# Hybrid pooling and latent-attention trunk on eight cores: the first two heads are prepared inside the projection of block 2, the norm runs at a fixed rate, the pooling products come one group later

## Chip, cores and metric

The kernel runs on all 8 cores of one Trainium2 chip. Each core works on its own requests and nothing is exchanged between cores. The metric is the device time of one launch in microseconds (us), that of the slowest core; lower is better.

## What is computed

The reference is a trunk of two layers. Cut to what matters here, layer 0 is:

```python
h = rms_norm(x, g) * (1 + scale) + shift            # adaLN: scale, shift from silu(cond) @ ada_w + ada_b
z = h @ w_in                                        # u (512) | cq (384) | ckv (256) | krope (32)
y_pool = pool(u) @ pool_w * pool_scale              # 4 groups, centred means over windows of 2, 4, 8, 16, minus the token
q = rms_norm((rms_norm(cq) @ w_uq) per head)        # 8 heads of 64 + 32; rotary on the last 32 for latent tokens
k, v = rms_norm(ckv) @ w_ukv                        # k: 64 + the shared 32 of krope, normalised per head
y = concat(y_pool, softmax(q k') v) @ w_out         # then x += gate * y, and a SwiGLU channel mixer
```

Layer 1 has a spatial-gating MLP in place of the mixer. A core holds 1536 tokens in three blocks of 512: block 0 is two prompts of 256 (context), blocks 1 and 2 are one latent sequence of 1024. The latent queries also see 512 cached context tokens, which the code calls key block 3. The outputs are the tokens, the normalised ckv and krope of the context.

## The kernel before

There is no compiler that orders the work. `Prog` emits instructions engine by engine in the order in which the Python code calls it, each engine runs its own in that order, and `op` (L184 to L206) attaches the semaphore waits that follow from tiles written and read. `_deps` adds one for a PSUM bank that two different engines read: the second waits for the first. All tiles lie in an arena with an allocator of its own (`new`, L50, and `drop`): a tile placed over a dropped one waits for the last use of that one. `Stream` (W) brings the weights in ten slots of 512 KB. Its DMAs are issued on the GpSimd (POOL) queue, each when `W.done` frees a slot, so they stand in one queue with POOL's arithmetic.

Order of the work: the adaLN weights and the norm of block 0; `inproj(b)` for the three blocks (L827); the preparation of heads 0 and 1 with the pooling of blocks 1 and 2; the attention of four pairs of heads (L1184), during which the next pair is prepared and 40 more pieces of `ada_w` are read and multiplied; the output projection; FFN, gMLP and FFN until the end. The work is interleaved with Python generators. A generator emits some instructions and yields, with a number that stands for the TensorE time it offers (the main one) or takes (a filler).

- `Norm.gen` (L576), 21 yields: a first one with no work; 8 squares (ACT, and POOL for every third) whose sums over the channels on TensorE follow three steps later in bank 7; the last three sums; the reciprocal root (ACT, two instructions); 8 steps of `apply`, one for each 128 channels: DVE multiplies into `xtmp` (for every fourth POOL does), ACT adds the shift and writes `hy`, which the projection of that block reads.
- `inproj(b)` has ten yields: two ckv projections, three cq projections, the krope projection (`pkr`), four tiles of u with tokens on the partitions (`u_tile`), each projection 8 matmuls of 512 columns, with the squares, sums and scalings of the two inner norms. It uses PSUM banks 0 to 5. It writes `ckvn[b]`, `cqn`, `kro` and `utok`.
- `pooling` (L910): for each of 4 groups of a block, 8 to 10 narrow matmuls of `utok` with a band matrix (the sum), its scaling out of PSUM into `pbf` (`evac`) with corrections of 8 columns at sequence ends (DVE, `icnt`), a yield, one matmul with `pool_w` (the product), its scaling into `hy`, a yield.
- `qkv(p, banks)` (L1001) prepares a pair of heads. There are six q units (192 columns for each of two token tiles; a copy into `qf`; square on POOL, `reduce` on DVE), after both units of a block `rnorm` (ACT), `rotate` (one DVE multiplication and up to five on POOL) and `turn` (8 transposes into `qT`), and for the four key blocks a k unit (2 matmuls, square on ACT, two copies into `kT`), a v unit (8 matmuls, one copy into `V`) and `sums`. `later(n, fn)` delays a step by n ticks; there is one tick for each yield.

`weave_in` (L956) gives `inproj(b)` its fillers, taken in turn against the debt: for block 0 the norm of block 1, for block 1 the norm of block 2 and the pooling of block 0, for block 2 nothing. Ahead of block b stands `drain(norms[b])`, which emits all that is left of its norm. Before the attention `weave` runs `qkv(0)` on banks 0 to 5 against the pooling of blocks 1 and 2 on banks 6 and 7 (`FB`), both scalings of the pooling on ACT. During the attention, `qkv(p + 1)` takes banks 6 and 7, which it shares with the `ada_w` pieces and the transposes of the outputs (`spread`).

## Time and profile before

| | us |
|---|---|
| median of 3 runs | 1262.86 |
| lowest of them | 1261.05 |
| the profiled execution | 1259.46 |
| its span, slowest core (core 5) | 1258.4 |
| spans of the eight cores | 1248.7 to 1258.4 |
| TensorE busy on core 5, share of the span | 1137.0, 90% |
| VectorE (DVE), ScalarE (ACT), GpSimd (POOL) busy | 480.3, 429.5, 227.8 |

All rows below are of core 5. In a timeline row the first number is the start in us, the second how long the merged instructions take from the first start to the last end; the end of a matmul includes the emptying of the array, so the next may start before it. Start to start is what a matmul costs. In brackets stands the idle time before the row and what ended it. `PEclk` is the granted TensorE clock as a share of 2.4 GHz.

### The profile page before, as it was taken

To read this page: it belongs to the slowest core of one execution; us is meant where nothing else is said; L and a number is where in the kernel's file an instruction comes from. 1 tells how busy PE (TensorE), PEld (TensorE's weight loads), DVE (VectorE), ACT (ScalarE), POOL (GpSimd) and SP (SyncE) were. 2 spreads that over 40 slices of the span, in tenths; PEclk is the share of its full clock that TensorE was granted. 3 is DMA by queue.
4 is the path that set the end of the run, shared out by engine and by line. 5 is a ranking of instruction groups with operands and counts; after the bars stand their busy time and mean duration, and the time that the engine had idled before them with its cause. 6 is when DMAs were issued, how large, how long until landed. Compare 5 with 4: busy or idle time off the path is not lost.

```text
span 1258.4 us, 17871 instructions; the slowest of 8 cores (1248.7 to 1258.4 us)
## 1 busy us (share of the span) xinstructions
PE 1137.0 (90%) x6857; PEld 547.9 (44%) x6857; DVE 480.3 (38%) x814; ACT 429.5 (34%) x669; POOL 227.8 (18%) x347
## 2 busy tenths in 40 slices
PE   2477678797889899999999999998899999999998
PEld 1233455554544344444444444444344444444443
DVE  0355673634136211152252253565622225125133
ACT  2455466665745511101101156543651110110100
POOL 3311452533213200000000022224310000000000
PEclk9988997868799899999999999998999999999999
DMA  9960318778991425225224206003533321410013
GB/s 187 239 110 1 59 30 141 112 118 130 155 167 36 67 38 92 39 35 84 34 34 84 51 1 109 1 1 49 98 55 67 68 35 34 84 17 1 1 76 126
DMA packets 24977, 90.04 MB, mean 72 GB/s; under 512 B 3392, under 2 KB 3776, under 8 KB 24128
## 3 DMA queue, kind: packets, MB, share of 16 engines
q0 software_dynamic: 21312, 77.10, 36.8%
q1 hardware_dynamic: 3584, 11.80, 2.8%
q8 instruction: 58, 0.95, 0.3%
q14 instruction: 23, 0.19, 0.1%
HBM read 153.85 MB, written 6.88 MB: 128 GB/s over the span
## 4 chain that ended last, share of the span: by engine, by line
PE 76%; DVE 7%; DMA 6%; ACT 5%; POOL 3%; issue 3%; POOLq 0%; ACTq 0%; DVEq 0%
PE pb L230 74%; DMA wslot<-w_in_u 3%; DMA wslot<-ada_w 3%; ACT pt L247 2%; DVE xtmp L268 2%; PE pb L228 2%; DVE kT L274 1%; POOL qs L251 1%; DVE xb L268 1%; DVE qf L274 1%; POOL qr L251 1%; ACT hy L247 0%; ACT xsq L247 0%; POOL qt L251 0%; DVE utok L251 0%
## 5 line engine op out<-in xcount | busy, mean ns | idle before, releaser
L230 PE MATMUL pb<-hb,wslotx 128*128 128x512 bf16 x1440 | 319.9, 379 | 0.0
L247 ACT ACTIVATE sg<-pb 128x512 f32<-128x512 f32 x132 | 78.7, 596 | 472.0 <-PE pb L230 472.0
L251 DVE TENSOR_TENSOR apart<-pb,sg 128x512 bf16<-128x512 f32 x132 | 91.3, 691 | 369.0 <-PE pb L230 346.2
L230 PEld LDWEIGHTS pb<-hb,wslotx 128*128 128x128 bf16 x1440 | 140.8, 98 | 170.0 <-issue 0.3
L268 DVE SCALAR_TENSOR_TENSOR xb<-pb,mod,xb 128x512 f32<-128x512 f32 x192 | 143.6, 749 | 143.1 <-PE pb L230 143.1
L230 PE MATMUL pb<-hb,wslot 128*128 128x512 bf16 x864 | 197.6, 385 | 0.0
L230 PE MATMUL pb<-apart,wslot 128*128 128x512 bf16 x768 | 167.1, 379 | 0.0
L247 ACT ACTIVATE pt<-pb,rk 128x1024 bf16<-128x1024 f32 (+1 forms) x128 | 118.9, 953 | 58.0 <-PE pb L230 57.2
L230 PEld LDWEIGHTS pb<-hb,wslot 128*128 128x128 bf16 x864 | 85.6, 99 | 104.9 <-issue 5.7
L230 PEld LDWEIGHTS pb<-apart,wslot 128*128 128x128 bf16 x768 | 75.1, 98 | 90.2
L230 PE MATMUL pb<-hy,wslot 128*128 128x512 bf16 (+1 forms) x336 | 82.4, 397 | 4.7 <-ACT hy L247 4.5
L230 PE MATMUL pb<-qT,kT 96*128 96x512 bf16 (+1 forms) x224 | 80.5, 449 | 1.6 <-issue 1.6
L268 DVE SCALAR_TENSOR_TENSOR xtmp<-xb,AA,xrs 128x512 f32<-128x512 f32 x72 | 62.5, 906 | 9.8 <-ACT xrs L247 9.4
L228 PEld LDWEIGHTS pb<-V,pt 128*128 128x128 bf16 x768 | 39.5, 109 | 59.7 <-issue 54.5
L247 ACT ACTIVATE xsq<-xb 128x512 bf16<-128x512 f32 x72 | 41.8, 621 | 65.4 <-PE pb L230 36.3
L230 PE MATMUL pb<-apart,wslotx 128*128 128x512 bf16 x288 | 62.5, 379 | 0.0
L230 PE MATMUL pb<-xsq,ones 128*128 128x512 bf16 x96 | 30.0, 405 | 32.0 <-ACT xsq L247 24.2
L228 PE MATMUL pb<-V,pt 128*128 128x65 bf16 x768 | 47.0, 212 | 12.2 <-ACT pt L247 10.7
L251 POOL TENSOR_TENSOR xtmp<-xb,xrs 128x512 f32<-128x512 f32 x24 | 33.6, 1402 | 124.6 <-ACT hb L247 85.4
L230 PEld LDWEIGHTS pb<-hy,wslot 128*128 128x128 bf16 (+1 forms) x336 | 33.4, 101 | 49.0 <-issue 14.8
L247 ACT ACTIVATE hb<-xtmp,mod 128x512 bf16<-128x512 f32 x54 | 37.6, 720 | 33.1 <-DVE xtmp L268 33.1
L230 PE MATMUL pb<-scT,wslot 128*128 128x2 bf16 x768 | 26.9, 165 | 21.5 <-DMA wslot<-ada_w 20.0
(130 smaller groups left out, 953.8 us busy)
## 6 DMA issues: line engine op xcount, KB each, us to landing
wslot<-ada_w POOLq DMA_DIRECT2D x48, 512.0 KB, 10.1
wslot<-ffn_wd POOLq DMA_DIRECT2D x16, 512.0 KB, 9.9
wslotx<-ffn_wu POOLq DMA_DIRECT2D x14, 512.0 KB, 10.6
wslotx<-ffn_wg POOLq DMA_DIRECT2D x12, 512.0 KB, 18.9
y<-xb SPq DMA_DIRECT2D x12, 512.0 KB, 2.7
wslot<-ffn_wg POOLq DMA_DIRECT2D x10, 512.0 KB, 7.4
xb<-x_in POOLq DMA_DIRECT2D x4, 1024.0 KB, 41.7
wslot<-ffn_wu POOLq DMA_DIRECT2D x8, 512.0 KB, 7.5
```

Of the source, the lines that this page charges most:

```text
L228: return self.op("pe", lambda g: g.matmul(out, lhsT, rhs, start=start, stop=stop, skip_group_check=True), [lhsT, rhs], [out], inc=inc)
L230: return self.op("pe", lambda g: g.matmul(out, lhsT, rhs, start=start, stop=stop), [lhsT, rhs], [out], inc=inc)
L247: return self.op("act", lambda g: g.activation(out=out, in_=in_, func=func, bias=bias, scale=scale), reads, [out])
L251: return self.op(e, lambda g: g.tensor_tensor(out=out, in0=in0, in1=in1, op=op), [in0, in1], [out])
L268: return self.op(e, lambda g: g.scalar_tensor_tensor(out=out, in0=in0, scalar=sc, in1=in1, op0=op0, op1=op1), reads, [out])
L274: return self.op(e, lambda g: g.tensor_copy(out=out, in_=in_), [in_], [out])
```

## The change

- `inproj(2)` now has `qkv(0)` as its filler: 12 of its steps, which are 12 of the 14 units. The tiles for it are made before block 2, and `qkv(0)` takes banks 6 and 7 there and banks 0 to 5 afterwards (`bk0`). For p = 0 `qf` is copied by ACT, no longer by DVE.
- `weave_in` and its debt are replaced by `together(main, n, parts)`: a part with k steps gives k/n steps for each of the n yields of main. The norm of block 1 runs at 26 steps on 10 yields, the norm of block 2 at 36 on 10, the pooling of block 0 at 9 on 10. The latter two are drained after block 1.
- `pooling` emits a product one group behind its sum where it has two banks. Of blocks 1 and 2 the `pbf` scaling moves from ACT to DVE; the scaling into `hy` stays on ACT.
- `qkv` is written as a list of units. The order is new for the later pairs too: q and k or v units alternate, where six q units stood ahead of all k and v units. The two `rotate` of a block come one tick apart, where both came in one. The copies of the rotary keys into `kT` (SP's DMAs) are issued for p = 0 after block 2.
- To make room in the arena: `Norm` has two `xrs` tiles for three blocks, `ckr_f` is dropped early, `in_kv` and `in_q0` are given back in the middle of block 2, and the allocator takes the tightest gap, no longer the first, in the whole kernel.

```diff
-        addr = gaps[-1][1] - nbytes if high else gaps[0][0]
+        addr = gaps[-1][1] - nbytes if high else min(gaps, key=lambda g: (g[1] - g[0], g[0]))[0]
...
-                self.rs = [new("xrs%d" % i, [128, 512], F32) for i in range(3)]
+                self.rs = [new("xrs%d" % i, [128, 512], F32) for i in range(2)]
+                self.rs.append(self.rs[0])
...
+            if b == 2:
+                W.done("in_kv")
+                W.done("in_q0")
             pq.append(proj(5, W.get("in_q1"), 0))
...
         def pooling(blocks, banks, step, evac):
+            late = collections.deque()
+            lag = len(banks) - 1
+            def product(b, g, pbf):
+                ps2 = P.bank(banks)
+                P.mm(ps2[:], pw[:, g, :], pbf[:])
+                evac[1](hy[b][:, g, :], ps2[:], vecs[:, 128 + g:129 + g])
...
-                    evac(pbf[:], ps[:], 1.0 / w)
+                    evac[0](pbf[:], ps[:], 1.0 / w)
...
                     yield step
-                    ps2 = P.bank(banks)
-                    P.mm(ps2[:], pw[:, g, :], pbf[:])
-                    evac(hy[b][:, g, :], ps2[:], vecs[:, 128 + g:129 + g])
-                    yield step
+                    late.append((b, g, pbf))
+                    if len(late) > lag:
+                        product(*late.popleft())
+                        yield step
...
+            while late:
+                product(*late.popleft())
+                yield step
...
-        for b in range(3):
-            drain(norms[b])
-            fill = collections.deque()
-            if b < 2:
-                fill.append(norms[b + 1])
-            if b > 0:
-                fill.append(pooling([b - 1] if b == 1 else [], (6,), 1.3, lambda o, i, sc: P.ts("dve", o, i, sc, None, ALU.mult)))
-            weave_in(inproj(b), fill)
...
-                    P.cp("dve", qf[:].rearrange("p a d -> p (a d)"), ps[:, 0:384])
-                    later(3 - u + 1, functools.partial(rotate, b, u, qf, qt, sr))
+                P.cp("act" if p == 0 else "dve", qf[:].rearrange("p a d -> p (a d)"), ps[:, 0:384])
                 later(1, functools.partial(reduce, ss, u, qs))
+                if u == 1:
+                    later(2, functools.partial(rnorm, ss, sr))
+                    for v in range(2):
+                        later(3 + v, functools.partial(rotate, b, v, qts[v][0], qts[v][1], sr))
+                    later(6, functools.partial(turn, b, [x[1] for x in qts]))
...
-            for kb in (3, 0, 1, 2):
...
+            order = [("q", 0, 0), ("q", 0, 1), ("k", 3), ("v", 3), ("q", 1, 0), ("q", 1, 1), ("k", 0), ("v", 0), ("k", 1), ("v", 1),
+                     ("q", 2, 0), ("q", 2, 1), ("k", 2), ("v", 2)] if p == 0 else [("q", 0, 0), ("k", 3), ("q", 0, 1), ("v", 3), ("q", 1, 0), ("k", 0), ("q", 1, 1), ("v", 0),
+                     ("q", 2, 0), ("k", 1), ("q", 2, 1), ("v", 1), ("k", 2), ("v", 2)]
+            for kind, *arg in order:
+                {"q": q_unit, "k": k_unit, "v": v_unit}[kind](*arg)
                 yield 0.5
                 tick()
...
+        def together(main, n, parts):
+            for i, _ in enumerate(main):
+                for g, k in parts:
+                    for _ in range((i + 1) * k // n - i * k // n):
+                        next(g, None)
+        drain(norms[0])
+        together(inproj(0), 10, [(norms[1], 26)])
+        drain(norms[1])
+        pool0 = pooling([0], (6,), 1.3, (on_dve, on_dve))
+        together(inproj(1), 10, [(norms[2], 36), (pool0, 9)])
+        drain(norms[2])
+        drain(pool0)
...
+        bk0 = [FB]
+        q0 = qkv(0, bk0)
+        together(inproj(2), 10, [(q0, 12)])
+        for key in ("in_u0", "in_u1", "in_q1"):
+            W.done(key)
...
-        q0 = qkv(0, (0, 1, 2, 3, 4, 5))
-        weave(q0, collections.deque([pooling([1, 2], FB, 0.5, lambda o, i, sc: P.act(o, i, AF.Copy, scale=sc))]), flush=True)
+        bk0[0] = (0, 1, 2, 3, 4, 5)
+        together(pooling([1, 2], FB, 0.5, (on_dve, on_act)), 16, [(q0, 9)])
+        drain(q0)
```

## Rows read from the trace of the kernel before

**Rows 1.** The page, granted TensorE clock in 40 slices of 31.5 us, tenths.

```profile
PEclk9988997868799899999999999998999999999999
```

**Rows 2.** Busy time by stretch: PE, PEld, DVE, ACT, POOL, clock, DMA share, GB/s.

```profile
80.90:107.70 26.80, 23.76 (x138) 11.22 (x134) 16.67 (x39) 12.71 (x23) 1.04 (x1) 1.00 0.10 15
107.70:136.80 29.10, 24.07 (x95) 9.43 (x96) 12.71 (x19) 15.06 (x24) 3.61 (x3) 0.82 0.04 5
136.80:166.40 29.60, 17.58 (x199) 13.64 (x197) 20.22 (x45) 15.49 (x31) 16.38 (x34) 0.88 0.34 63
166.40:358.80 192.40, 158.08 (x2085) 98.72 (x2085) 81.84 (x208) 131.31 (x167) 71.36 (x140) 0.81 0.78 122
358.80:1258.40 899.60, 879.87 (x4112) 399.62 (x4112) 328.97 (x459) 224.44 (x379) 109.34 (x130) 0.99 0.29 53
```

**Rows 3.** TensorE's waits, 107.7 to 166.4 us: total, times, longest.

```profile
PE pb L230 <- DVE pbf L251: 9.2, 5, 3.1
PE pb L230 <- ACT hy L247: 4.5, 3, 3.3
```

**Rows 4.** TensorE's timeline where block 2 begins.

```profile
106.87 0.81 PE L230 MATMUL pb<-xsq,ones 128*128 128x512 bf16 x3
110.97 1.91 PE L230 MATMUL pb<-hy,wslot 128*128 128x512 bf16 x3 [3.29 <-ACT hy L247]
113.51 2.42 PE L230 MATMUL pb<-hy,wslot 128*128 128x512 bf16 x4 [0.63 <-ACT hy L247]
116.51 6.12 PE L230 MATMUL pb<-hy,wslot 128*128 128x512 bf16 x17 [0.58 <-ACT hy L247]
```

**Rows 5.** TensorE's timeline, matmuls at full clock, one after the other.

```profile
142.32 0.66 PE L230 MATMUL pb<-wslot,cqn 128*128 128x192 bf16 x6
142.81 0.66 PE L228 MATMUL pb<-band,utok 128*128 128x132 bf16 x10
143.33 0.66 PE L230 MATMUL pb<-wslot,cqn 128*128 128x192 bf16 x6
...
182.10 0.63 PE L239 MATMUL pb<-ident,qt 128*96 128x128 bf16 x8 [1.17 <-DVE kT L274]
182.57 0.61 PE L230 MATMUL pb<-wslot,ckvn 128*128 128x128 bf16 x8
183.02 0.60 PE L230 MATMUL pb<-qT,kT 96*128 96x512 bf16 x2
...
359.59 15.70 PE L230 MATMUL pb<-hy,wslot 128*128 128x512 bf16 x72
```

**Rows 6.** Groups, 60 to 170 us: line, engine, operation, count, busy us, mean ns.

```profile
L268 DVE SCALAR_TENSOR_TENSOR xtmp<-xb,AA,xrs 128x512 f32<-128x512 f32 x12 | 9.6, 839 | 0.4 <-ACT xrs L247 0.3
L274 DVE COPY qf<-pb 128x384 f32<-128x384 f32 x8 | 4.4, 547 | 1.1 <-PE pb L230 1.1
L259 DVE TENSOR_SCALAR pbf<-pb 128x512 bf16<-128x512 f32 x4 | 2.8, 692 | 2.9 <-PE pb L228 2.9
L247 ACT ACTIVATE pbf<-pb 128x512 bf16<-128x512 f32 x8 | 4.7, 588 | 1.5 <-PE pb L228 1.3
```

**Rows 7.** TensorE's waits during the attention, 166.4 to 358.8 us.

```profile
PE pb L228 <- ACT pt L247: 10.7, 28, 0.8
PE pb L239 <- DVE kT L274: 6.3, 5, 1.5
PE pb L230 <- DVE kT L274: 4.1, 5, 1.1
```

**Rows 8.** Busy time in four stretches of the attention, columns as in group 2.

```profile
193.00:206.00 13.00, 12.84 (x132) 7.08 (x129) 4.12 (x14) 8.25 (x10) 1.59 (x3) 0.50 1.04 159
244.00:269.00 25.00, 23.94 (x256) 13.23 (x255) 4.91 (x18) 17.45 (x19) 2.12 (x4) 0.50 0.94 149
306.00:332.00 26.00, 24.78 (x263) 13.87 (x264) 3.87 (x16) 18.07 (x23) 3.41 (x7) 0.50 1.00 158
333.00:358.00 25.00, 18.46 (x276) 9.62 (x272) 1.76 (x8) 22.62 (x21) 6.34 (x12) 1.00 0.98 155
```

More of the change, by code:

```diff
@@ L825, in build @@
         key_sums(3)
+        drop(ckr_f)
         def inproj(b):
@@ L1004, in qkv @@
             kT, qT, V, rk = d["kT"], d["qT"], d["V"], d["rk"]
-            for hl in range(2):
-                P.dma("sp", kT[64:96, hl, :], kro[64:96, :], "kro%d" % (p % 2))
+            if p > 0:
+                rotary_keys(p)
             lag = collections.deque()
@@ L1023, in turn @@
             def turn(b, qts):
-                ps = P.bank(banks).bitcast(BF16)
+                ps = P.bank(banks[0]).bitcast(BF16)
                 for hl in range(2):
@@ new lines, in q_unit @@
+            def q_unit(b, u):
+                if u == 0:
+                    qst[b] = (ssr.next(), ssr.next(), [])
+                ss, sr, qts = qst[b]
+                ps = P.bank(banks[0])
+                for i in range(2):
+                    t = 4 * b + 2 * u + i
+                    P.mmg(ps[:, i * 192:(i + 1) * 192], [(cqn[:, kc, t * 128:(t + 1) * 128], wuq[kc][:, p * 192:(p + 1) * 192]) for kc in range(3)])
+                qf = qfr.next()
+                qs = qsr.next()
+                qt = qtr.next()
+                qts.append((qf, qt))
+                P.cp("act" if p == 0 else "dve", qf[:].rearrange("p a d -> p (a d)"), ps[:, 0:384])
+                P.tt("pool", qs[:], qf[:], qf[:], ALU.mult)
+                later(1, functools.partial(reduce, ss, u, qs))
+                if u == 1:
[3 more added lines that the diff above has]
+                    later(6, functools.partial(turn, b, [x[1] for x in qts]))
@@ L1077, in qkv, with sums @@
             ksb = new("ksb", [128, 16, 2], F32)
-            pend = None
-            def sums():
-                kb, sq = pend
-                ps = P.bank(banks)
+            def sums(kb, sq):
+                ps = P.bank(banks[0])
                 for i in range(4):
@@ L1086, in sums, with k_unit @@
                 P.tt("dve", ksb[:, kb * 4:kb * 4 + 4, :], ps[:, 0:8].rearrange("p (a b) -> p a b", b=2), k_bc, ALU.add)
-            for kb in (3, 0, 1, 2):
-                ps = P.bank(banks)
-                lw = [wukv[:, kc, p * 256:p * 256 + 128] for kc in range(2)]
-                P.mmg(ps[:], [(lw[kc], ckvn[kb][:, kc, :]) for kc in range(2)])
+            def k_unit(kb):
+                ps = P.bank(banks[0])
+                P.mmg(ps[:], [(wukv[:, kc, p * 256:p * 256 + 128], ckvn[kb][:, kc, :]) for kc in range(2)])
                 sq = sqk.next()
@@ L1095, in qkv, with v_unit, krstd @@
                     P.cp("act" if p == 0 and hl == 1 else "dve", kT[0:64, hl, blk(kb)], ps[hl * 64:hl * 64 + 64, :])
[L1096 to L1098 removed]
+                later(2, functools.partial(sums, kb, sq))
+            def v_unit(kb):
+                ps = P.bank(banks[0])
                 for i in range(4):
[L1100 to L1101 removed]
+                    P.mmg(ps[:, i * 128:(i + 1) * 128],
+                          [(ckvn[kb][:, kc, i * 128:(i + 1) * 128], wukv[:, kc, p * 256 + 128:p * 256 + 256]) for kc in range(2)])
                 P.cp("dve", V[:, kb * 4:kb * 4 + 4, :, 0:64], ps[:].rearrange("p (t h d) -> p t h d", t=4, h=2))
+            def krstd():
+                P.act(ksb[:], ksb[:], AF.Ln, bias=epsc[:, 3:4])
+                P.act(rk[:], ksb[:], AF.Exp, scale=-0.5)
+                drop(ksb)
+            qst = {}
+            order = [("q", 0, 0), ("q", 0, 1), ("k", 3), ("v", 3), ("q", 1, 0), ("q", 1, 1), ("k", 0), ("v", 0), ("k", 1), ("v", 1),
[3 more added lines that the diff above has]
+                {"q": q_unit, "k": k_unit, "v": v_unit}[kind](*arg)
                 yield 0.5
                 tick()
[L1105 to L1112 removed]
+            later(2, krstd)
             while lag:
@@ L1115, in qkv @@
                 tick()
+        def together(main, n, parts):
[3 more added lines that the diff above has]
+                        next(g, None)
+        on_dve = lambda o, i, sc: P.ts("dve", o, i, sc, None, ALU.mult)
+        on_act = lambda o, i, sc: P.act(o, i, AF.Copy, scale=sc)
+        drain(norms[0])
[5 more added lines that the diff above has]
+        drain(pool0)
+        N.close()
+        drop(*held)
+        wukv = W.get("ukv")
+        wuq = [W.get("uq0")[:, 0, :], W.get("uq0")[:, 1, :], W.get("uq1")[:, 0, :]]
+        kvq = [new_kvq(0)]
+        qfr = Ring([new("qf%d" % i, [128, 4, 96], F32) for i in range(5)])
+        qsr = Ring([new("qs%d" % i, [128, 4, 96], F32) for i in range(2)])
+        qtr = Ring([new("qt%d" % i, [128, 4, 96], BF16) for i in range(6)])
+        qrr = Ring([new("qr%d" % i, [128, 2, 4, 32], F32) for i in range(2)])
+        sqk = Ring([new("sqk%d" % i, [128, 512], BF16) for i in range(2)])
+        ssr = Ring([new("ss%d" % i, [128, 8], F32) for i in range(4)])
+        bk0 = [FB]
[3 more added lines that the diff above has]
+            W.done(key)
+        drop(*sqb.t, *rsb.t, *t2k.t, sqkr, ropek)
+        rotary_keys(0)
+        ptr = Ring([new("pt%d" % i, [128, 1024], BF16) for i in range(3)])
+        rdr = Ring([new("rd%d" % i, [128, 4], F32) for i in range(2)])
         def ada_gen():
@@ L1218, in before @@
             drain(nxt[0])
-            nxt[0] = qkv(p + 1, FB) if p < 3 else iter(())
+            nxt[0] = qkv(p + 1, [FB]) if p < 3 else iter(())
         debt = 0.0
```

56 lines of the change are left out of this document (5 added, 51 removed).

## The prediction

> **What bounds the kernel now.** I read the clock line of the page first, then the busy time by stretch, then TensorE's waits in the stretches that the change touches, and last the timeline where they fall. The last 899.6 us, from the output projection on, have TensorE busy for 879.87 at a clock of 0.99 [rows 2], and the change leaves their order alone: they are fixed. The clock line has its low digits from the third slice to the eleventh [rows 1]. What can move is three stretches ahead of the attention and the attention itself. From 80.9 to 107.7 us runs the projection of block 1 (26.8 us, clock 1.00). From 107.7 to 136.8 runs block 2 (29.1 us, clock 0.82), from 136.8 to 166.4 the first preparation with the pooling (29.6 us, TensorE busy 17.58), and then 192.4 us of attention at a clock of 0.81 [rows 2].
>
> Two waits stand out in the 58.7 us from 107.7 on [rows 3]. TensorE waits 4.5 us for `hy`: the norm of block 2 isn't ready when block 1 is, since two fillers shared the debt, and `drain` emits what is left of it in one piece. TensorE waits 9.2 us for `pbf`: a pooling product stands directly behind its own sum, and TensorE takes its queue in order, so the q and k units behind it stand too. After the first of the two waits the matmuls of block 2 run at half clock: 17 in 6.12 us, 0.36 each [rows 4], where 72 take 15.70, 0.22 each [rows 5].
>
> **What TensorE must do.** Prices, start to start: a matmul of 512 columns 15.70/72 = 0.218; a q unit 142.81 - 142.32 = 0.49; a pooling sum 143.33 - 142.81 = 0.52; a turn 182.57 - 182.10 = 0.47; a v unit 183.02 - 182.57 = 0.45; a k unit two matmuls of 512, 0.44 [rows 5]. I put 0.12 for four sums of two columns (estimate, a quarter of the 8 narrow matmuls of a v unit). The projection of a block has 80 matmuls of 512 columns and 5 for its inner norms: 85 x 0.218 = 18.5.
> - Block 1: 18.5, with 8 norm sums 1.7 and the pooling of block 0, 4 x (0.52 + 0.22) = 3.0: 23.2.
> - Block 2, with 12 steps of `qkv(0)`: 18.5, six q units 2.9, three k and three v units 2.7, two turns 0.9, three sums 0.4: 25.4.
> - Pooling stage: 8 x 0.74 = 5.9, one k and one v unit 0.9, one turn 0.5, one sum 0.1: 7.4.
>
> Together 56.0, where 85.5 pass now. A gain of 29.5 is thus the bound from above for this part. None of the arithmetic goes away; only idle time and half clock do.
>
> **Block 1 becomes longer.** At 3.6 steps a yield the norm is through its squares in three yields and through its 8 `apply` in the fourth to sixth: up to 4 in one yield, 3 of them on DVE at 0.84 [rows 6], 2.5 us, beside the scalings of the block and of the pooling, against some 2.2 us of TensorE. So DVE falls behind by about 4 us there. The pooling of block 0 has one bank (6), its product waits for DVE's `pbf` and its next sum for DVE's `hy`: these stand behind the `apply` in DVE's queue, and all later projections stand behind them in TensorE's. I count two such waits of 1.5 to 2.2 us and two of about 0.6: 5, on top of 23.2 and of some 1.3 that stay as they are: 29.5. Bounds: 25 if DVE's other idle time takes it all up; 33 if most of the norm's rest, which now shows as 9 us of delay between 107.7 and 116.5 [rows 4], returns inside the block. Over the block DVE has 16.67 + 6 x 0.84 = 21.7 us of work in it, so it doesn't bound the whole.
>
> **Block 2 takes in the preparation.** What goes: the wait of 3.29 with its 0.63 and 0.58, and the half clock, 24 matmuls at 0.14 more than 0.22 each, 3.4 us [rows 4]. What comes: 6.9 us of units. On two banks each unit waits until the one two before it is out of PSUM; a unit lasts a yield of 2.4 us, and a k unit needs a square on ACT and two copies one after the other, about 2 us. So most waits are covered. A turn stands behind POOL's rotations, about 2.2 us each for latent tokens, and these have two ticks: I give 1 us of waiting for that, 2 for the banks. 25.4 + 3.1 = 28.5. Bounds: 26 and 32. The copies of `qf` on ACT take 6 x 0.55 from DVE. If ACT is late, TensorE's squares of `sqb` are, and they are of the next inner norm only. POOL's queue holds three weight DMAs at the end of block 2, as now; their pieces are wanted by the attention, 14 us later.
>
> **The pooling stage.** With the product one group behind, TensorE no longer waits for the `pbf` just made, but sums and products still alternate over two banks, so that every sum has the same bank as the sum before. A group costs the sum 0.52, its scaling on DVE 0.69 [rows 6], a correction and the hand-overs 0.3: 1.5; eight make 12. DVE has some 5 us of `qkv(0)` to do in between, of which 3 fit beside the sums that TensorE makes meanwhile: I take 14. Bounds: 12 and 18. `pbf` on ACT costs 0.59 [rows 6], so the move itself is a loss of 0.1 a group, made up by the saved hand-over between ACT's scaling and DVE's correction. The key copies on SP are issued at the end of block 2 and have the whole stage to land.
>
> Sum: 29.5 + 28.5 + 14 = 72.0 for 85.5, a gain of 13.5; from the bounds 25 + 26 + 12 and 33 + 32 + 18, between 22.5 and 2.5. DVE's total of 49.6 over the three stretches [rows 2] goes up by 8 x 0.69 and down by 6 x 0.55, to 51.8, still below 72.
>
> **The attention.** The diff also reorders the later pairs. Now a k unit, a v unit and a turn come close together on banks 6 and 7, and TensorE waits for the copies of `kT` for 6.3 + 4.1 = 10.4 us [rows 7]; the 6.3 are all turns, as the one of 1.17 ahead of 182.10 [rows 5]. In the new order the turns come due at ticks 8, 12 and 16, behind v units, and three of four k units are followed by a q unit. The turns' waits should go; the 4.1 stay, since an `ada_w` piece between two units takes a bank as well. In these stretches TensorE is the late one, so a wait saved there is time saved: 6. Bounds: -3 (the waits turn up behind `qf` instead, which has a DVE copy too, and prep ends later by its tail of 2 yields) and 16 (below). The weight stream is not in the way: 192 us carry 40 pieces, 4.8 us each.
>
> **Clock in the attention.** Three stretches of 13, 25 and 26 us run at half clock with TensorE busy 95% and more of the time, and in the timeline each comes soon after a pair's k units; in the last 25 us, at full clock, TensorE idles 6.5 of 25 and keeps the clock [rows 8]. At half clock a step costs about 1.6, in comparable steps at full clock 1.25 (estimate, from 13 and 7 steps that I counted in the timeline): 64 us at half clock cost 14. If what costs the clock is the waits of the k units, part of the 14 comes back. The Trainium skill (TensorE: Matmul & The Clock Gate, "A second HAM failure mode: psum-queue depth-cycling") says that a kernel that cycles through PSUM banks, with short idle times between groups of matmuls, loses and regains the clock again and again. By that rule the low stretches stay, for the short waits stay, and the attention gives 6 at most; the last stretch of rows 8 speaks against it. I leave the clock as it is in the sum and make its return a rival.
>
> **Allocator and the rest.** Tightest gap for first gap changes which freed tile a new one waits for. After the attention TensorE needs its first FFN weights about 40 us later, so a DMA that starts up to ten us later is hidden; without that cover it would show as a wait for `wslotx`. Two `xrs` for three blocks: block 2's root waits for block 0's last `apply`, a whole block earlier. Nothing for both, bounds -2 and 2.
>
> **Sum.** 1259.46 (profiled execution, span 1258.4 and 1.1 around it) - 13.5 - 6 = 1240. The median of the runs shown is 3.4 above the profiled execution, the lowest 1.6 above; I put 2 on it: **1242**.
>
> **The rivals.**
> - *The idle time only moves (19%).* DVE's backlog in block 1 and the two-bank chains keep what the waits gave up: front 5, attention 2, time 1254. For it: DVE's 20.22 of 29.6 us [rows 2] already come from such chains. Against it: each of the two waits of rows 3 has a cause that the diff removes.
> - *The attention's clock comes back (17%).* 10 of the 14 us, with 19.5: 1232; with a good front stage 1226. For it: the low stretches follow the k units. Against it: they might as well follow from the load that comes later, and the rule above.
> - *Slower (4%).* In block 1, or behind a turn in block 2, TensorE waits 3 us and more in one piece, as ahead of 110.97, and the clock falls to 1.2 GHz there and is not regained because the waits recur. Block 2 and the pooling stage with half of block 1 are 44 us of TensorE work at full clock. Doubled, less the 12 us of waits that it swallows, that costs 32 and gives 1242 + 32 = 1274. It decides from 27 us of work at half clock on, where the 19.5 are used up. For it: 3.29 us of waiting did cost the clock [rows 4]. Against it: the longest single wait I count is 2.2.
> - *It doesn't do what it says (5%).* Block 2's norm is drained late all the same, as ACT and DVE take their queues in order; then front 2 and attention 2, time 1257.
> - *As forecast (55%)*, own range 1233 to 1250.
>
> **How the numbers follow.** 1225 is the rival of the clock with a good front stage, 1256 reaches past the idle time that only moves; outside lie the slower case, half of the one that does nothing and the ends of the others. 2% is 25 us, about what a measurement of this kernel can tell from no change: the line is at 1237.6. Below it lie the rival of the clock and a quarter of the forecast: 0.30. Above 1288 lies little of the slower case, but its price is uncertain: 0.03. The rest, 0.67, is within.
>
> **What the profile after would show.** Right: no `hy` wait of over 1 us where block 2 begins, clock 1.00 through block 2; first scores of the attention near 153 us, not 166.5; block 1 longer by 2 to 3 us with waits for DVE's `pbf` and `hy`; the `pbf` wait in the pooling stage replaced by sums that wait for DVE's `pbf` of the sum before, under 1 us each; no turns that wait for `kT`. Wrong: scores later than 160; attention longer than 190; a new wait for POOL's `qt` of some us. The forecast is wrong as a whole if the part from 358.8 on changes by more than 3.

## The result, and the profile after

The changed kernel takes 1272.82 us against 1261.05 in the same comparison (medians of five runs each). In some launches the cores of one die ran longer at a lower clock; the ratios leave these launches out, the medians include them. The ratio is 1.009, 95% interval 1.0076 to 1.0103: slower by under 2%, but clearly slower. The forecast was 1242, with a range of 1225 to 1256: wrong in sign and outside the range. The slowest core's span is 1272.9 us where it was 1258.4.

The page's clock line answers to [rows 1]. The fourth digit, with block 2 in it, is 9 where it was 8. The sixth to the eleventh, most of the attention, are 7, 8, 7, 6, 9 and 5, where they were 9, 7, 8, 6, 8 and 7:

```profile
PEclk9989978769599999999999999999999999999999
```

Busy time by stretch on core 6, the slowest, columns as in [rows 2]. The cuts are the key sums of blocks 0, 1 and 2, the first score and the first transposes behind the attention. (In [rows 2] the two cuts after blocks 1 and 2 lie 0.9 and 0.6 us behind the key sums.)

```profile
81.20:112.50 31.30, 24.07 (x134) 11.11 (x136) 20.04 (x45) 19.72 (x33) 3.76 (x4) 1.00 0.08 13
112.50:139.10 26.60, 24.44 (x158) 12.84 (x160) 14.83 (x28) 14.30 (x28) 6.99 (x13) 1.00 0.00 1
139.10:163.60 24.50, 13.85 (x135) 10.34 (x136) 15.42 (x34) 8.46 (x16) 9.21 (x21) 0.82 0.47 78
163.60:372.20 208.60, 166.33 (x2074) 106.62 (x2084) 79.43 (x207) 131.00 (x165) 68.60 (x138) 0.75 0.68 113
372.20:1272.90 900.70, 875.90 (x4029) 399.81 (x4112) 330.24 (x461) 224.41 (x379) 110.25 (x132) 0.99 0.28 53
```

Three things are to be seen. Block 2 follows block 1 at full clock, with the preparation of pair 0 inside. The stage behind it still lasts 24.5 us, with TensorE busy for 13.85. And the attention, 192.4 us before at a clock of 0.81 [rows 2], is 208.6 here at 0.75. The last stretch is 900.7 for 899.6: it didn't change.

The wait where block 2 began [rows 4] is gone. This is TensorE's timeline around that place, with the first q unit of pair 0 behind the first projection:

```profile
112.43 0.24 PE L230 MATMUL pb<-ones,sqkr 128*128 128x1 bf16 x4
112.54 1.89 PE L230 MATMUL pb<-hy,wslot 128*128 128x512 bf16 x8
114.61 0.66 PE L230 MATMUL pb<-wslot,cqn 128*128 128x192 bf16 x6 [0.19 <-DVE hy L259]
```

TensorE's waits in block 1, 81.2 to 112.5 us: total, times, longest. Before, the stretch had only 1.7 for `hy` and some for the band's DMA.

```profile
PE pb L230 <- DVE pbf L251: 2.8, 3, 1.2
PE pb L228 <- DVE hy L259: 2.3, 2, 1.6
PE pb L230 <- ACT hy L247: 0.9, 1, 0.9
PE pb L230 <- ACT rsb L247: 0.6, 1, 0.6
```

The same from the key sums of block 2 to the first score, 139.1 to 163.6 us. The 9.2 us for `pbf` [rows 3] are 2.2 + 0.6 now, but a copy of `V`, a turn and `hy` have taken their place:

```profile
PE pb L230 <- DVE V L274: 3.6, 1, 3.6
PE pb L239 <- POOL qt L251: 2.5, 3, 1.8
PE pb L228 <- DVE pbf L251: 2.2, 4, 0.8
PE pb L230 <- ACT hy L247: 1.5, 2, 1.2
PE pb L230 <- DVE pbf L251: 0.6, 1, 0.6
```

The longest of them, on TensorE and on DVE. The q unit that starts at 142.99 needs the bank that the copy of `V` empties, and DVE does the rotary keys of block 2 first:

```profile
142.99 0.66 PE L230 MATMUL pb<-wslot,cqn 128*128 128x192 bf16 x6 [3.57 <-DVE V L274]
139.40 1.54 DVE L268 SCALAR_TENSOR_TENSOR t2k<-pb,vecs,ropek 32x512 f32<-32x512 f32 x2
140.97 0.68 DVE L251 TENSOR_TENSOR kro<-t2k,t2k 32x512 bf16<-32x512 f32 x1
141.69 0.42 DVE L251 TENSOR_TENSOR qt<-qf,ss 128x256 bf16<-128x256 f32 x1
142.15 0.69 DVE L274 CAST V<-pb 128x512 bf16<-128x512 f32 x1
```

And in the attention, 163.6 to 372.2 us, against [rows 7]. The turns no longer wait for `kT`, they wait for POOL:

```profile
PE pb L228 <- ACT pt L247: 9.6, 27, 0.7
PE pb L239 <- POOL qt L251: 8.9, 6, 2.6
PE pb L230 <- DVE kT L274: 6.6, 6, 1.2
PE pb L230 <- DMA wslot<-ada_w: 4.2, 5, 1.5
PE pb L239 <- DVE mod L251: 3.4, 4, 1.9
PE pb L230 <- DVE ksb L251: 2.4, 4, 0.7
```

To compare kernels I took the same cuts on all eight cores and averaged: from the key sums of block 0 to those of block 1, from there to those of block 2, from there to the first score, and the attention from its first to its last exponential. "Half clock" is twice the attention's length times (1 - its mean granted clock), the time it would be at 1.2 GHz if it is at 2.4 otherwise; "busy" and "waits" are TensorE's in the attention. The runs are described further below.

| kernel | block 1 | block 2 | stage behind | attention | half clock | busy | waits | ratio to before (95%) |
|---|---|---|---|---|---|---|---|---|
| before | 26.2 | 29.2 | 30.7 | 187.4 | 55 | 150.5 | 34.9 | |
| changed | 31.1 | 26.6 | 24.6 | 201.5 | 85 | 158.9 | 40.7 | 1.009 (1.0076, 1.0103) |
| e1 old pairs | 31.1 | 26.6 | 24.6 | 187.3 | 53 | 149.6 | 35.6 | 0.9956 (0.9940, 0.9971) |
| e2 new pairs alone | 26.3 | 29.3 | 30.5 | 200.1 | 79 | 156.6 | 41.8 | 1.0093 (1.0065, 1.0121) |
| e3 q first | 31.3 | 26.6 | 24.7 | 181.8 | 45 | 146.3 | 33.5 | 0.9925 (0.9908, 0.9943) |
| e4 late turn | 31.1 | 26.6 | 24.6 | 200.4 | 84 | 156.6 | 41.8 | 1.006 (1.0043, 1.0077) |
| e5 norm rate alone | 31.1 | 19.0 | 30.6 | 186.6 | 49 | 147.9 | 37.1 | none |
| e6 product lag alone | 26.5 | 29.3 | 30.1 | 184.7 | 39 | 144.9 | 38.2 | 0.9984 (0.9971, 0.9998) |
| e8 allocator alone | 26.0 | 29.2 | 30.3 | 185.3 | 43 | 145.9 | 37.5 | 0.9986 (0.9975, 0.9997) |
| e9 alternating, q early | 31.1 | 26.7 | 24.6 | 199.8 | 87 | 159.6 | 38.2 | 1.005 (1.0035, 1.0065) |
| e10 q late, in twos | 31.3 | 26.6 | 24.6 | 192.2 | 80 | 158.6 | 31.3 | 0.999 (0.9968, 1.0011) |
| e11 slower norm | 29.6 | 26.7 | 24.5 | 181.1 | 39 | 144.7 | 34.2 | 0.9902 (0.9887, 0.9918) |
| e12 ten steps | 31.0 | 24.7 | 23.9 | 181.1 | 43 | 146.4 | 32.6 | 0.9899 (0.9881, 0.9917) |
| e13 four banks | 31.3 | 26.7 | 22.1 | 180.9 | 39 | 144.7 | 34.5 | 0.9907 (0.9889, 0.9924) |
| e14 extra matmuls | 31.2 | 26.6 | 24.6 | 204.9 | 56 | 166.2 | 37.3 | 1.0126 (1.0099, 1.0152) |
| e15 qf on ACT | 31.1 | 26.7 | 24.7 | 201.6 | 90 | 160.2 | 39.5 | 1.0076 (1.0058, 1.0094) |
| e16 combined | 29.3 | 24.7 | 23.5 | 180.8 | 38 | 144.0 | 34.9 | 0.989 (0.9874, 0.9905) |
| e17 pair 0 late | 29.2 | 19.1 | 34.3 | 183.5 | 48 | 147.4 | 34.1 | 0.994 (0.9921, 0.9960) |

So the part ahead of the attention went from 86.1 to 82.3 us, a gain of 3.8, and the attention from 187.4 to 201.5, a loss of 14.1. The attention's loss is 8.4 us more of busy TensorE and 5.8 more of waiting. No arithmetic was added, so I put the 8.4 down to the 30 us more at half clock. Kernels with the same attention code (before, e5, e6, e8) lie between 184.7 and 187.4, with 39 to 55 us at half clock: about 3 us of length and 16 us of half clock are what one profile each leaves open, and 201.5 and 85 lie well outside. The five kernels with the q units first in the later pairs (e3, e11, e12, e13, e16) lie between 180.8 and 181.8.

### The profile page after: what moved, and what is told of

Its sections match the earlier page's. It is cut to its first block, busy times and chain, and to the rows that moved or that the text cites. A ratio compares the mean times of both kernels' runs of the same rounds, so it can differ in the third digit from the quotient of the medians.

```text
span 1272.9 us, 17738 instructions; the slowest of 8 cores (1259.7 to 1272.9 us)
## 1 busy us (share of the span) xinstructions
PE 1137.6 (89%) x6753; PEld 556.0 (44%) x6857; DVE 480.4 (38%) x816; ACT 427.1 (34%) x667; POOL 225.4 (18%) x347
## 4 chain that ended last, share of the span: by engine, by line
PE 75%; DMA 8%; DVE 7%; ACT 5%; issue 3%; POOL 2%; POOLq 0%; ACTq 0%; DVEq 0%
PE pb L230 72%; DMA wslot<-ada_w 4%; DMA wslot<-w_in_u 3%; ACT pt L247 2%; DVE xtmp L268 2%; PE pb L228 1%; DVE kT L274 1%; PE pb L239 1%; POOL qr L251 1%; ACT hy L247 1%; DVE xb L268 1%; ACT hb L247 1%; ACT xsq L247 0%; POOL qt L251 0%; ACT rsb L247 0%
## 5 line engine op out<-in xcount | busy, mean ns | idle before, releaser
L230 PE MATMUL pb<-qT,kT 96*128 96x512 bf16 (+1 forms) x224 | 84.2, 468 | 0.0
L230 PE MATMUL pb<-hy,wslot 128*128 128x512 bf16 (+1 forms) x327 | 78.4, 390 | 2.5 <-ACT hy L247 0.9
L228 PE MATMUL pb<-V,pt 128*128 128x65 bf16 x768 | 47.1, 212 | 11.1 <-ACT pt L247 9.6
L230 PE MATMUL pb<-xsq,ones 128*128 128x512 bf16 x94 | 29.3, 405 | 31.0 <-ACT xsq L247 23.1
L247 ACT ACTIVATE hb<-xtmp,mod 128x512 bf16<-128x512 f32 x54 | 37.6, 720 | 34.2 <-DVE xtmp L268 34.2
## 6 DMA issues: line engine op xcount, KB each, us to landing
wslot<-ada_w POOLq DMA_DIRECT2D x48, 512.0 KB, 10.4
```

What stands on the lines that cost most here:

```text
L228: return self.op("pe", lambda g: g.matmul(out, lhsT, rhs, start=start, stop=stop, skip_group_check=True), [lhsT, rhs], [out], inc=inc)
L230: return self.op("pe", lambda g: g.matmul(out, lhsT, rhs, start=start, stop=stop), [lhsT, rhs], [out], inc=inc)
L247: return self.op("act", lambda g: g.activation(out=out, in_=in_, func=func, bias=bias, scale=scale), reads, [out])
```

## The experiments

**e1: the old preparation for pairs 1 to 3.** `qkv_old` is `qkv` as in the kernel before.

```diff
-            nxt[0] = qkv(p + 1, [FB]) if p < 3 else iter(())
+            nxt[0] = qkv_old(p + 1, FB) if p < 3 else iter(())
```

> The changed kernel with the preparation of pairs 1 to 3 as it was before (six q units first, both rotations in one tick); pair 0, the norm, the pooling and the allocator stay changed. Theory A (the new order of the later pairs makes the attention longer): the attention's first three pairs go back from about 56, 57 and 53 us to 50, 52 and 50, its whole from 202 to about 188, the waits for POOL's qt from 8 us to under 1, the time from 1272 to about 1258. Theory B (what comes ahead of the attention, its earlier start on the same weight stream, makes it longer): it stays above 198 and the time at 1270. Theory C (tiles placed over others by the tightest gap): as B.

**e2: the new preparation alone, on the kernel before.**

```diff
-            nxt[0] = qkv(p + 1, FB) if p < 3 else iter(())
+            nxt[0] = qkv_new(p + 1, [FB]) if p < 3 else iter(())
```

> The kernel before with only the new preparation of pairs 1 to 3. Theory A: the start of the attention stays near 167 us, the attention grows from 187 to about 202, the time to about 1275. Theories B and C: nothing moves by more than 3 us, time 1261.

Measured: 1256.95 and 1273.66 us, the attention 187.3 and 200.1, waits for POOL's `qt` 0.2 and 8.2. Theory A holds both ways. The loss sits in the new preparation of the later pairs, which the change's own name doesn't mention; e3 narrows it to the order of the units. Theories B and C fall: with all of the front changed (e1) the attention is the old one, and e8 below adds the allocator's rule alone.

**e3: only the list of pairs 1 to 3, q units first.**

```diff
-[("q", 0, 0), ("k", 3), ("q", 0, 1), ("v", 3), ("q", 1, 0), ("k", 0), ...]
+[("q", b, u) for b in range(3) for u in range(2)] + [(kv, kb) for kb in (3, 0, 1, 2) for kv in "kv"]
```

> The changed kernel with one list changed: in pairs 1 to 3 the six q units stand first again, then k and v; rotations one tick apart and all else as changed. If theory A acts through the place of the last q units (block 2's rotations and its turn fall into the tail, whose yields are short, so the turn waits for POOL): waits for POOL's qt fall from 8 us to about 1, the waits for kT come back to some 11, the attention to about 190, the time to about 1260. If it acts through the rotations one tick later, waits for qt stay at half or more and the time above 1267.

Measured: 1253.11 us, ratio 0.9925. The attention is 181.8, 20 us shorter than with the changed list and 5.5 shorter than with the old code, whose two rotations came in one tick: waits for `kT` 6.9, for `qt` next to none. So the order of the list is the cause of the loss, and the tick between the rotations isn't.

**e4: only the turn of block 2 later in pairs 1 to 3.**

```diff
-                    later(6, functools.partial(turn, b, [x[1] for x in qts]))
+                    later(6 if b < 2 or p == 0 else 10, functools.partial(turn, b, [x[1] for x in qts]))
```

> The changed kernel with only the turn of block 2 later in pairs 1 to 3: 10 ticks behind its last q unit, where it was 6. If the hurried last turn is the whole cost: waits for POOL's qt fall to under 2 us, attention 202 to about 190, time about 1260. If it is the smaller part, and the alternation of units (more waits for kT and for the ada_w pieces' mod on two banks) the larger: qt waits fall the same but the time stays above 1265.

Measured: 1270.59 us, attention 200.4, the second reading. The waits for `qt` are gone, and others stand in their place: 11.1 us for weight DMAs in the mean of the cores, where the changed kernel has 2.8. TensorE's waits in the attention of e4, core 2:

```profile
PE pb L230 <- DMA wslot<-ada_w: 13.2, 5, 4.0
PE pb L228 <- ACT pt L247: 9.5, 29, 0.7
PE pb L230 <- DVE kT L274: 8.5, 7, 1.7
```

POOL's timeline in the changed kernel (core 6) shows why both waits are one matter:

```profile
191.81 0.82 POOL L251 TENSOR_TENSOR qs<-qf 128x384 f32<-128x384 f32 x1
192.57 0.60 POOL L220 DMA_DIRECT2D wslot<-ada_w  x1
198.79 0.39 POOL L251 TENSOR_TENSOR qf<-qf,ss 128x128 f32<-128x128 f32 x1 [5.62 <-DVE qt L251]
199.26 1.04 POOL L251 TENSOR_TENSOR qr<-qf,ropeq 128x128 f32<-128x128 f32 x2
200.38 0.72 POOL L251 TENSOR_TENSOR qt<-qr 128x64 bf16<-128x64 f32 x2
201.32 0.60 POOL L220 DMA_DIRECT2D wslot<-ada_w  x1 [0.22 <-issue]
201.94 0.41 POOL L251 TENSOR_TENSOR qf<-qf,ss 128x128 f32<-128x128 f32 x1
202.42 0.86 POOL L251 TENSOR_TENSOR qr<-qf,ropeq 128x128 f32<-128x128 f32 x2
203.37 0.72 POOL L251 TENSOR_TENSOR qt<-qr 128x64 bf16<-128x64 f32 x2
204.30 1.13 POOL L220 DMA_DIRECT2D wslot<-ada_w  x2 [0.21 <-issue]
```

and TensorE's at the same time:

```profile
201.35 0.28 PE L239 MATMUL pb<-ident,qt 128*96 128x128 bf16 x2 [0.96 <-POOL qt L251]
204.23 0.85 PE L239 MATMUL pb<-ident,qt 128*96 128x128 bf16 x6 [2.60 <-POOL qt L251]
```

The last rotations of a pair begin with a wait of 5.62 us, and the weight DMAs emitted meanwhile stand behind them in POOL's queue: between 192.57 and 201.32 none is issued. The turn's wait covers the missing pieces; take it away, and TensorE waits for the pieces.

**e9 and e10: where the last q unit stands, and whether units alternate.**

```diff
 # e9
+[("q", 0, 0), ("k", 3), ("q", 0, 1), ("q", 1, 0), ("v", 3), ("q", 1, 1), ("q", 2, 0), ("k", 0), ("q", 2, 1), ("v", 0), ("k", 1), ("v", 1), ("k", 2), ("v", 2)]
 # e10
+[("q", 0, 0), ("q", 0, 1), ("k", 3), ("v", 3), ("q", 1, 0), ("q", 1, 1), ("k", 0), ("v", 0), ("k", 1), ("v", 1), ("q", 2, 0), ("q", 2, 1), ("k", 2), ("v", 2)]
```

> The changed kernel with another list for pairs 1 to 3: q and k or v units still alternate, but the last q unit is the 9th of 14, where it is the 11th in the changed kernel and the 6th with the q units first. If the lateness of the last q unit is what costs (rotations, weight DMAs behind them on POOL, the turn): attention about 184 us, time about 1256. If the mixing of units costs: attention about 196, time about 1266.

> The changed kernel with the list of pair 0 for all pairs: two q units, then a k and a v, and the last q unit the 12th of 14. If lateness costs: attention 200 us or more, waits for POOL's qt 8 us or more, time 1272 or more. If the alternation one by one costs: attention about 188, time about 1259.

Measured: ratios to before of 1.005 and 0.999; attention 199.8 and 192.2, against 181.8 with q first and 201.5 as changed. Neither reading comes out alone. Lateness without one-by-one alternation costs 10 us (e10 against e3); alternation with the last q unit two places earlier keeps all but 1.7 of the loss. (e9 alternates in part only: two of its q units follow another one directly.) e9 has waits for `qt` of 1.2 only, but 6.1 for the weight DMAs, and total waits of 38.2; its busy time is 159.6, 13.3 above e3's. e10 has the fewest waits of all, 31.3, and waits for `qt` of 4.4, half of what lateness should have brought; its loss of 10.4 against e3 is 12.3 us more of busy time, less 2.2 of waits. What all three slow lists share is the half clock, 80 to 87 us against 45.

**e14: extra matmuls.** The results stay the same, since each unit overwrites the bank.

```diff
+            def fill(ps):
+                if p > 0:
+                    for _ in range(2):
+                        P.mm(ps[:], wukv[:, 0, p * 256:p * 256 + 128], ckvn[3][:, 0, :], inc=False)
...                                  # in q_unit, k_unit and v_unit, behind ps = P.bank(banks[0])
+                fill(ps)
```

> The changed kernel with two extra matmuls of 512 columns ahead of each unit of pairs 1 to 3, into the bank that the unit overwrites: 84 of them, 18 us of TensorE time at full clock; the results stay the same. If the alternating order loses the clock because it thins TensorE's work, the extra work buys part of it back: time at half clock in the attention 85 us to under 65, attention longer by 8 us or less (201.5 to at most 209). If the half clock has another source: half clock as before or more, attention longer by 18 us and more.

**e15: the copies of `qf` on ACT in all pairs.**

```diff
-                P.cp("act" if p == 0 else "dve", qf[:].rearrange("p a d -> p (a d)"), ps[:, 0:384])
+                P.cp("act", qf[:].rearrange("p a d -> p (a d)"), ps[:, 0:384])
```

> The changed kernel with the copies of qf on ACT in pairs 1 to 3 too. If the alternating order costs because DVE has each k unit's two copies ahead of the next unit's qf on two banks: waits of TensorE for DVE's kT and mod from 13 us to under 9, attention 201 to about 194. If lateness on POOL and the clock hold it: attention 199 or more; and ACT, which makes the exponentials, may add to it.

Measured: ratios to before of 1.0126 for e14 and 1.0076 for e15, the first reading of e14 and the second of e15. In e14 the half clock falls from 85 to 56 us and the attention grows by 3.4 us, for 18 us of added matmuls. These are the first 30 us of pairs 0, 1 and 2 on core 6, in which the next pair is prepared. First the changed kernel, then e14; the sixth number after the length is the clock:

```profile
164.50:194.50 30.00, 24.67 (x315) 18.30 (x317) 17.12 (x40) 18.05 (x27) 12.70 (x24) 0.76 0.36 56
222.20:252.20 30.00, 23.55 (x290) 16.73 (x290) 16.85 (x40) 17.48 (x26) 13.00 (x26) 0.74 0.53 90
281.10:311.10 30.00, 23.57 (x326) 16.74 (x327) 18.59 (x42) 18.73 (x28) 13.85 (x27) 0.83 0.54 91
```

```profile
163.60:193.60 30.00, 24.72 (x308) 16.68 (x307) 16.00 (x37) 16.98 (x26) 11.48 (x23) 0.93 0.30 50
223.60:253.60 30.00, 24.34 (x326) 16.63 (x325) 18.05 (x42) 17.50 (x26) 14.19 (x27) 1.00 0.54 90
278.90:308.90 30.00, 24.91 (x346) 16.76 (x345) 18.16 (x42) 18.29 (x28) 13.95 (x27) 1.00 0.55 91
```

TensorE is shown as busy for about the same time in both, but in the changed kernel part of that is the same matmuls at half speed. Averaged over the three pairs and eight cores this clock is 0.95 before, 0.84 changed, 0.93 in e3, 0.80 in e9, 0.87 in e10 and 0.97 in e14. So more work for TensorE takes the half clock out of the preparation. It isn't a thing of the front (e2 has 79 us of it) nor of the copies of `qf` on DVE (e15: waits for `kT` and `mod` together 14.3 against 13.4, half clock 90). What in the order brings it about is not shown. TensorE's waits in these 30 us, summed over the three pairs, are 20.4 us in 34 pieces before, 18.4 in 33 in e3, 19.3 in 26 in the changed kernel, 20.0 in 26 in e9 and 14.3 in 24 in e10; neither their sum nor their number puts the clocks in order. Nor is it the whole: these 90 us hold 9 us of half clock before, 29 changed, 13 in e3 and 5 in e14, so of the 40 us between the changed kernel and e3 only 16 lie there. The other 24 fall behind the preparation, e14 leaves them, and no run explains them. As a remedy the extra work is worth nothing: by the ratios 4.5 us more in all.

**e5 and e6: two parts of the front alone.** e5 takes the fixed rates into the kernel before, with no filler in block 2; e6 the new `pooling` with its evacuations.

```diff
 # e5
-            weave_in(inproj(b), fill)
...
+        together(inproj(0), 10, [(norms[1], 26)])
...
+        together(inproj(1), 10, [(norms[2], 36), (pool0, 9)])
...
+        drain(inproj(2))
 # e6
-pooling([1, 2], FB, 0.5, lambda o, i, sc: P.act(o, i, AF.Copy, scale=sc))
+pooling([1, 2], FB, 0.5, (lambda o, i, sc: P.ts("dve", o, i, sc, None, ALU.mult), lambda o, i, sc: P.act(o, i, AF.Copy, scale=sc)))
```

> The kernel before with only the fixed rate of the norms (26 and 36 steps on 10 yields, the pooling of block 0 at 9); block 2 has no filler, pooling and preparation as before. Theory F1 (the norm's 9 us of delay is paid back in block 1 by DVE's burst, some 5 us): block 1, from the key sums of block 0 to those of block 1, 26 to 31 us, block 2 29.5 to 20.5, the first score 4 us earlier, time about 1257. Theory F2 (ACT and DVE take it up beside TensorE): block 1 stays at 27, the first score 8 us earlier, time about 1253.

> The kernel before with only the pooling's products one group behind their sums and its pbf scaling of blocks 1 and 2 on DVE. Theory F3 (the 9.2 us of waits for pbf are TensorE's alone): the stage from the key sums of block 2 to the first score 31 to 24 us, time about 1255. Theory F4 (the stage is held by the chain sum, scaling, sum on two banks and by DVE, which gets the scaling on top): 31 to 29 or more, time 1260.

Measured for e5: block 1 longer by 4.9 and block 2 shorter by 10.2, as F1 says. Only two of its launches can be compared, 1251.43 and 1255.46 us, too few for an interval and nearer to F2's time. Block 2 and the stage behind it on core 0:

```profile
111.50:130.50 19.00, 18.59 (x91) 8.46 (x92) 8.24 (x14) 8.43 (x15) 0.60 (x1) 1.00 0.09 13
130.50:161.00 30.50, 17.85 (x198) 14.36 (x199) 20.45 (x46) 15.75 (x31) 16.37 (x34) 0.88 0.34 58
```

The part ahead of the attention is 80.7 us here, where the whole change has 82.3: the norm's rate alone brings 5.4, and the other edits of the front give 1.6 of it back. Beside e5, pair 0 in block 2 makes that block longer by 7.6 and the stage shorter by 6.0 only.

For e6: ratio 0.9984, the stage 30.1 where it was 30.7. F4 holds. TensorE's timeline in e6, core 0, two sums in the middle of the stage:

```profile
151.03 0.66 PE L228 MATMUL pb<-band,utok 128*128 128x1 bf16 x10 [2.40 <-DVE pbf L251]
156.04 0.67 PE L228 MATMUL pb<-band,utok 128*128 128x2 bf16 x10 [2.81 <-DVE pbf L251]
```

These products no longer wait for their `pbf` (3.0 us of such waits are left in the stage, mean of the cores, of 8.5), but the next sum waits for the bank that the same `pbf` is read from, and DVE gets to that late: 5.3 us. Most of the wait was moved by one instruction.

**e8: the allocator's rule alone, on the kernel before.**

```diff
-        addr = gaps[-1][1] - nbytes if high else gaps[0][0]
+        addr = gaps[-1][1] - nbytes if high else min(gaps, key=lambda g: (g[1] - g[0], g[0]))[0]
```

> The kernel before with only the allocator's rule changed (tightest gap). Theory C (placement costs time by waits on other tiles): more than 3 us slower. Otherwise: 1261, front stages 26, 29 and 31 us and attention 187, each within 2 us.

Measured: ratio 0.9986, front stages and attention within 2.1 us of before: no loss, so theory C falls.

**e11, e12 and e13: three sizes of the front, each on e3.**

```diff
 # e11
-        together(inproj(1), 10, [(norms[2], 36), (pool0, 9)])
+        together(inproj(1), 10, [(norms[2], 26), (pool0, 9)])
 # e12
-        together(inproj(2), 10, [(q0, 12)])
+        together(inproj(2), 10, [(q0, 10)])
...
-        together(pooling([1, 2], FB, 0.5, (on_dve, on_act)), 16, [(q0, 9)])
+        together(pooling([1, 2], FB, 0.5, (on_dve, on_act)), 16, [(q0, 11)])
 # e13
-            lag = len(banks) - 1
+            lag = min(len(banks) - 1, 1)
...
-        bk0[0] = (0, 1, 2, 3, 4, 5)
-        together(pooling([1, 2], FB, 0.5, (on_dve, on_act)), 16, [(q0, 9)])
+        bk0[0] = (0, 1, 2, 3)
+        together(pooling([1, 2], (4, 5, 6, 7), 0.5, (on_dve, on_act)), 16, [(q0, 9)])
```

> The changed kernel with the q units first in pairs 1 to 3 (e3), and the norm of block 2 at 26 steps on 10 yields in place of 36. If the burst of the norm on DVE and ACT is what makes block 1 longer: 31.3 to about 28.5 us, the rest the same, time about 1250 against 1253 of e3. If it is the work as such, block 1 stays at 31.

> e3 with 10 steps of pair 0 in block 2, where it has 12: the last two q units, which wait at the end of block 2 for DVE's copy of V and need the last scaled cq, stand in the pooling stage on six banks. If the squeeze at the end of block 2 costs: the last front stage 24.7 to about 22 us, the block 25.5, time about 1250. If the stage is held by DVE and the two banks of the pooling: no change in the sum of the two within 1 us.

> e3 with the pooling of blocks 1 and 2 on four banks (4 to 7) and pair 0 on banks 0 to 3 there; products still one group behind. Theory F4a (each sum waits for the scaling of the sum before on the same bank): the last front stage 24.7 to about 20 us, time about 1249. Theory F4b (DVE's queue and the hurried last turn hold it): 24 or more, time 1253.

Measured, in ratios 0.9902, 0.9899 and 0.9907 against 0.9925 of e3: each helps by 2.3 to 3.3 us, though its interval overlaps with e3's. The norm at 26 gives back 1.7 of the 5 us in block 1; whether the rest is what is left of the burst or the work itself isn't shown. Two steps fewer in block 2 save 1.9 there and 0.8 behind. Four banks take 2.6 from the stage, half of what I expected, and leave the 3.6 us wait for `V` and the turn's for POOL.

**e16 and e17: all of it together, and together without the main edit.** e16 is e3 with e11, e12 and e13. e17 takes from it the preparation inside block 2:

```diff
-        together(inproj(2), 10, [(q0, 10)])
+        together(inproj(2), 10, [])
...
-(on_dve, on_act)), 16, [(q0, 11)])
+(on_dve, on_act)), 16, [(q0, 21)])
```

> e3, e11, e12 and e13 together: q units first in the later pairs, the norm of block 2 at 26 on 10, 10 steps of pair 0 in block 2, the pooling of blocks 1 and 2 on four banks. If their gains add up: front stages about 29.5, 24.7 and 21.5, attention 181, time about 1243. If they share the same waits: 1248.

> e16 with pair 0 wholly in the pooling stage (21 steps on 16 yields) and block 2 without a filler. If moving the preparation into block 2 is worth its place: block 2 24.7 to 19, the last front stage 23.5 to 31 or more, time 1250 against 1247. If the units cost as much TensorE time and waiting in block 2 as they free in the stage behind: the sum of the two stays within 1.5 us of 48.2 and the time within 2.

Measured: 1247.19 us, 0.989 (0.9874 to 0.9905), the fastest kernel here and 2% under the changed one; and 0.994 (0.9921 to 0.9960) for e17. Block 2 and the stage behind take 48.2 us in e16 and 53.4 in e17. Against e17 the edit that gives the change its name is worth 5.2 us of front and some 6 of the whole. But e17 places pair 0 badly: its stage is 34.3 us with 9.8 of waits for POOL's `qt` in the turns (mean of the cores), where the old interleaving of e5 needs 30.6. Block 2 and the stage of e5 take 49.6, and beside those e16 gains 1.4, though e5 differs from it in the pooling too. The gains of e11 to e13 don't quite add up: the front is 77.5 against 82.6 in e3, 5.1 less, where the three alone gave 1.8, 3.0 and 2.5; by the ratios e16 gains 4.4 us on e3, where they gave 8.5 together.

## Why the prediction was wrong

**Where the waits are, and that the norm's delay and most of the `pbf` waits would go.** Right. So were the end (900.7 for 899.6 us) and the allocator (e8). All three signs of being wrong that I had set for the profile appeared: first scores at 163.6 us and not near 153, an attention over 190, and new waits for POOL's `qt`.

**Block 2: 29.1 to 28.5.** Measured 29.2 to 26.6, but not because the preparation is covered there. With the norm in time and no preparation the block takes 19.0 (e5), so the preparation costs 7.6 in it. And I had put all 12 steps into the block: two of the six q units and one of the two turns are emitted behind its key sums and fall into the next stage, 1.5 us of work by my prices. (A slip besides: waits of 1 and 2 us went into the sum as 3.1.)

**Block 1: 26.8 to 29.5.** Measured 26.2 to 31.1. The mechanism held: waits for DVE's `pbf` and `hy` in the places named, 5.1 us in all (I had counted 5). Two terms were too small: TensorE's own work, 24.07 us for 23.2, and what else waits, 2.0 us for ACT's `rsb`, `hy` and others for 1.3. It lies within the bounds.

**The pooling stage: 14, bounds 12 to 18.** Measured 24.6. This step failed by its size, and its bound too. I costed a group by the chain of its own instructions on two banks, 1.5 us, and took DVE as free when a `pbf` was due. The first group comes only after 3.6 us of waiting for a copy of `V` that stands behind the rotary keys of block 2 on DVE, and the last turn waits for POOL. The work moved here from block 2 adds 1.5 us. And the sum had no term for the clock: 0.75 in the mean of the cores (0.82 on core 6), where it was 0.87, which is part of why TensorE was busy for 14.8 us with work of 7.4 + 1.5. The rows of before had the sign of it: DVE was busy for 20.22 of 29.6 us there, and still TensorE waited for it. e6 shows it by itself: 0.6 us for waits of 9.2 that I took as removed.

**The attention: a gain of 6, bounds -3 and 16.** This is the step that turned the sign: measured a loss of 14.1. I looked at the turns' waits for `kT`, found that the new order puts no turn behind a k unit, and counted 6. The turns' waits for `kT` did go, 6.1 us in the mean of the cores; the other waits for `kT` rose from 5.8 to 8.0. I did not ask what else stands at the new places. Two things do. The last q unit comes 11th in place of 6th; its turn falls in the tail, whose yields are short, behind two rotations on POOL and with the weight DMAs behind those: 8.0 us of waits for `qt` where there were 0.1, 2.8 for the DMAs where there were 1.0. Those for `mod` rose too, from 2.5 to 5.4. And the first 30 us of each pair, at a clock of 0.95 with six q units in front, run at 0.84. Half clock in the attention went from 55 to 85 us, 20 of these 30 in those first stretches, and TensorE's busy time rose by 8.4.

**The clock.** I took the low stretches as following the k units' waits and thus as something that fewer waits could only improve, and left the clock out of the sum; as a rival I had only its return. The Trainium skill (TensorE: Matmul & The Clock Gate, "A second HAM failure mode: psum-queue depth-cycling") says that short idle times between groups of matmuls bring the clock up and down. I set the last stretch of [rows 8] against it. The runs agree with it in that the low stretches stayed, and e14 took half clock away by adding work. But I drew from it only that they would stay as they are, and they grew from 55 to 85 us; and the waits alone don't foretell it, for e10 has the fewest, 31.3 us, and 80 us at half clock.

**The rivals.** The slower one had the right engine state, half clock, and the wrong place, the front; I gave it 4%. That the idle time only moves (19%) is what the front did: a gain of 3.8 in place of 13.5, and this rival said 5.

What stays open: how the 20 us between the changed list and e3's divide between lateness and alternation, and how either costs the clock. e9 and e10 each change both a little, and the three slow lists lie within 10 us of each other. The list alone can't part the two: with six q units the last of them stands sixth only if all six stand first. And the kernel before, with its q units first as well, has an attention 5.6 us longer than e3's; which of the remaining differences in the preparation gives that wasn't tried.

## What to carry to other kernels

Read every edit of a diff for what it moves in each queue, those beside its stated aim above all: here a reordered list of fourteen units, the same work in the same loop, cost 14 us and outweighed the rest. When a wait is moved off one instruction, ask which one next needs the same bank or the same engine, and cost that with the engine's queue as it is, not with the chain of its own instructions. Run each edit of a change by itself: one of the three in the front, the norm's rate, brought more than all of them together. In this kernel it paid to keep the q units together and to finish early what others have to wait for.

## What the runs showed of the hardware

Two extra matmuls ahead of each of 42 units, 18 us at full clock, made the attention longer by 3.4 us only (e14), since the time at half clock fell from 85 to 56 us. The busy shares alone don't show it: in the two kernels TensorE is busy for 23.3 and 24.5 of the first 30 us, at clocks of 0.84 and 0.97. Busy time at a low clock looks like a well-used engine.
